# Two modulation part sums moved from product stages to two norms on TensorE

## The chip, the cores and the metric

The kernel runs on one core of a Trainium2 chip. The metric is the device time of one execution in microseconds (us), taken as the median of several runs. One core has a matmul engine (TensorE, called PE in the profile, with its weight loads shown apart as PEld), a vector engine (VectorE, DVE), a scalar engine (ScalarE, ACT), GpSimd (POOL) and SyncE (SP). The last two mostly issue transfers here.

## The reference, cut to what matters

Two transformer blocks of two layers each work on 256 tokens of width 1024; layer 0 has 256 context tokens beside them. Every layer is modulated by a vector computed from a condition:

```python
m_lat = jnp.split((cond_lat @ mod_w[layer] + mod_b[layer])[:, None, :], 6, axis=-1)   # first block
h_lat = modulate(rms_norm(x, norm_g[layer, 0]), m_lat[0], m_lat[1])                   # h * (1 + scale) + shift
...
x = x + m_lat[5] * swiglu(modulate(rms_norm(x, norm_g[layer, 1]), m_lat[3], m_lat[4]), ffn_w_in[layer], ffn_w_out[layer])
...
mod = c_act @ w_ada[l] + b_ada[l]                                                     # second block
```

Each of the four modulation matrices is 1024 x 6144. This is a product of one or two row vectors with a large matrix, and none of it depends on the tokens. All of it can be done at any time before the layer that needs it.

## The kernel before, in words

Every engine's program is written out by hand, in the order in which that engine runs it; semaphores join them. The token products fill PE nearly all the time.

The modulation is cut into twelve groups, three of 2048 columns for each of four layers (`MOD_GROUPS`, L220). Group 0 is made by PE from the weights. For groups 1 to 11 the matrix comes in 88 slabs of 128 rows, each 1 MB. DVE multiplies each slab with its piece of the condition and adds it up in an accumulator of 128 x 2048 (`mod_slabs`, L2966). What is left is the sum over the 128 partitions. PE makes it in `mod_sum` (L1430): products of a selecting matrix with the four quarters of the accumulator, 32 rows each, into one PSUM bank. ACT copies that bank to `mod_rows` (L2288). PE turns it in `mod_turn` (L1420) by four transposes, and ACT copies 16 columns out (L2297). From group 4 on, a sum waits for the columns of the group before it, since the bank and `mod_rows` are shared.

Where PE runs the sums and turns is set by three small tables:

- In the first feed-forward's down product, twelve chunks with seven products each, group 5 is summed at chunk 3 and group 6 at chunk 7 (`MOD_DOWN_SUM`). Each is turned one chunk later. ACT copies them from inside the squares for the next norm (L2661 to L2665).
- In the odd layer, jobs are counted: 12 value units (0 to 11), 8 query products, 8 key products. Groups 7 to 11 are summed after jobs 1, 4, 8, 20 and 25 (`MOD_SUM_AFTER`), and each is turned after the next job. Before the retention scores PE waits for all twelve columns (L2034).

A norm on PE (`norm`, L1466) adds up squares by products with a matrix of ones. ACT then makes the inverse root (Ln, Exp), DVE scales the eight blocks of x, ACT adds the shift, and the first products of the next stage wait for these blocks one by one. While the chain runs, PE makes constant products whose result nobody reads (`spare`, L1453), 3 of width 512 where the norm has 512 tokens and 2 where it has 256. Each f32 product of the program appears as two instructions in the trace.

The value units (`retention_values`) and the feed-forward (`seven_products`) use a seven-product scheme of the Strassen kind: 1, 2, 5, 6, 1 of the next, 7, and so on. ACT copies the results of products 1, 6 and 7 out, because product 6 is added on top of product 1 in the same PSUM bank, and product 7 on top of that. So product 6 of a unit waits for the copy of product 1 (L2604 in the feed-forward, L2686 in the value units), and product 7 for the copy of product 6 (L2609 and L2696). The weights come over the SP queue in a ring of tiles, each load waiting for the products that used the tile before.

Of the kernel before, what the change touches and what calls it, by code (L numbers as in the profile page):

```python
# [219 lines left out]
MOD_GROUPS = [(layer, g) for layer in range(4) for g in range(3)]  # L220
MOD_SUM_AFTER = {"even": (13,), "odd": (1, 4, 8, 20, 25)}
MOD_EARLY = 8
SP_SLABS = 36
MOD_UP_SUM, MOD_DOWN_SUM = {9: 3, 19: 4}, {3: 5, 7: 6}
MOD_UNITS, MOD_ODD = (1, 2, 3, 2, 3, 2, 3, 2, 0, 0, 0, 0), 14
# [5 lines left out]


DOWN_SLABS = (2, 2, 0, 3, 3, 0, 3, 3, 0, 2, 2, 0)

# [228 lines left out]
def first_then_second_block(nc, a, out):  # L463
# [3 lines left out]
    with ExitStack() as ctx:  # L467
# [575 lines left out]
        def _(pe):  # L1043
# [413 lines left out]

            def feed_forward_norm(use, width, name, f):

                def between():  # L1460
                    pe.wait_ge(st_e, 28 * f + 23)
                    nc.tensor.matmul(acc[:, 3, 0:256], ones, fconst[:, 0:256], start=True, stop=True)

                norm(use, width, name, (st_e, 28 * f + 22), between)

            def norm(use, width, name, free=None, between=None):  # L1466

# [13 lines left out]
                if use:  # L1481
                    spare(mx[:, 1, :], 3 if width == 512 else 2)
                fresh[0] = use
# [261 lines left out]

            def seven_products(f, use, width, up_name, down_name, ffT, mods=False, params=None, final=False):

# [78 lines left out]
                for q in range(1, KF):  # L1826
# [9 lines left out]
                    if mods and q in MOD_UP_SUM:  # L1836
                        mod_sum()
                    product3(q - 1)
                    product7(q)
# [188 lines left out]
            seven_products(0, 1, 512, "ffn0", "down0", ffT4, mods=True)  # L2028
            feed_forward_norm(2, 512, "norm2", 0)
            own.n = 0  # L2030
            retention_values(2)
            for lo in (256, 256, 0, 0):
                by_feature(4, lo, 512, where="odd")
            pe.wait_ge(mod_c, len(MOD_GROUPS))  # L2034
            def ret_scores(h):
# [25 lines left out]
            quadrants("ret_out", roT, 8, *turned_back("ret_oT", 2))  # L2061
            norm(3, 256, "norm3", (out_e, 28 * OUT_USE["ret_out"] + 23))
            seven_products(1, 3, 256, "ffn1", "down1", ffT2, params=0)


# [169 lines left out]
        def _(act):  # L2235
# [352 lines left out]

            def feed_forward(f, width, mods=False):

# [7 lines left out]
                for q in range(KF + 1):  # L2598
# [18 lines left out]
                    if mods and q in MOD_UP_SUM:  # L2617
                        mod_sum()
                    if q:
                        act.wait_ge(st_c00, pair0 + q)  # L2620
                        nc.scalar.activation(g0[:, 1 - b, 0:w], g0[:, 1 - b, 0:w], ACT.Silu).then_inc(st_g0, 1)
# [34 lines left out]
            def down0_done(block):  # L2656

                p = block // 2
                if block % 2 == 0:
                    if p == 1:  # L2660
                        mod_sum()  # L2661
                        mod_turn()
                    if p == 2:
                        mod_sum()
                        mod_turn()  # L2665
                    down_done(0, 512, block)
# [13 lines left out]
            for q in range(units + 1):  # L2680
# [6 lines left out]
                if q == 0:  # L2687
                    shifted(2, 512, first=10)
                if q >= 1:
                    act.wait_ge(rv_x, q)  # L2690
# [42 lines left out]
            norm(3, 256, "norm3", quadrants_done("ret_out", 8))  # L2733
            feed_forward(1, 256)

# [205 lines left out]
        def _(dve):  # L2941
# [811 lines left out]
            quadrants("ret_out", 2, roT, 8, 1, lambda: weights_summed(KF + 12, pl.tile["ffn1"], 4))  # L3753
            dve.wait_ge(mod_c, 12)

            def layer_params(l):

                dve.wait_ge(par_sb, 2 * l + 2)
                link(V.tensor_tensor(mb[:, l, 0, :], modc[:, 2 + l, 0, :], vcols[:, 48 * l + 128:48 * l + 176], ALU.add))
# [404 lines left out]
```

## Time and profile before

| | |
|---|---|
| median of 3 runs | 2548.81 us (2548.07 to 2548.89) |
| the profiled execution, whole | 2547.73 us |
| its span | 2545.9 us |
| PE busy | 2474.6 us, 97% |
| DVE busy | 1696.6 us, 67% |
| ACT busy | 659.2 us, 26% |

The span is the time from the first to the last instruction that the profiler saw; the whole execution has 1.8 us around it. Times in the timelines are counted from the start of the span. An entry in brackets gives how long the engine was idle before a row and what ended that.

### The profile page before, as it was taken

How to read it: one execution, taken by the hardware profiler on the slowest of the kernel's cores; microseconds unless marked ns; L12 is line 12 of the kernel's file. 1: busy time of each engine (PE TensorE's matmuls, PEld its weight loads, DVE VectorE, ACT ScalarE, POOL GpSimd, SP SyncE). 2: the span in 40 equal slices, each digit the busy share in tenths (PEclk: the TensorE clock that was granted, in tenths of full speed). 3: DMA queues.
4: the chain of work that ended last, by engine and by line, in shares of the span. 5: the costliest groups of instructions: out<-in, count | busy, mean ns of one | idle time of the engine just before them, and what ended most of it. 6: DMA issues, size and time to landing. Idle time of an engine off the chain costs nothing.

```text
span 2545.9 us, 41380 instructions
## 1 busy us (share of the span) xinstructions
PE 2474.6 (97%) x16822; PEld 2022.4 (79%) x16822; DVE 1696.6 (67%) x3326; ACT 659.2 (26%) x1768; POOL 73.2 (3%) x96
## 2 busy tenths in 40 slices
PE   6999899999999999999999999999999999999999
PEld 3544448888888886599998877869999877868999
DVE  4967767655877645466675777647776667648785
ACT  3145512111102111112212153333321135333320
POOL 0000000000000001100000001100000000110000
PEclk9999999999999999999999999999999999999999
DMA  8531115555575868335654424135653433124563
GB/s 342 189 117 42 51 34 182 151 179 166 190 272 176 288 213 312 89 114 160 174 167 150 152 80 133 68 112 143 171 174 129 156 124 108 68 90 143 166 179 121
DMA packets 342654, 386.80 MB, mean 152 GB/s; under 512 B 8111, under 2 KB 285191, under 8 KB 330177
## 3 DMA queue, kind: packets, MB, share of 16 engines
q1 hardware_dynamic: 330896, 320.89, 40.3%
q0 software_dynamic: 8832, 57.26, 6.3%
q10 hardware_dynamic: 2736, 6.01, 0.6%
q8 instruction: 134, 2.20, 0.4%
q14 instruction: 56, 0.45, 0.1%
HBM read 383.08 MB, written 1.05 MB: 151 GB/s over the span
## 4 chain that ended last, share of the span: by engine, by line
PE 83%; DVE 9%; ACT 3%; issue 3%; DMA 2%; ACTq 0%; DVEq 0%; SPq 0%
PE acc L1072 33%; PE mx L1072 16%; PE acc L1123 9%; PE acc L1111 7%; PE acc L1200 5%; PE acc L1696 2%; PE acc L1645 1%; PE mx L2054 1%; DMA ring<-in_odd_w_in 1%; DVE arena L4077 1%; PE mx L1505 1%; DVE hT L3017 1%; PE mx L2041 1%; PE mx L2113 1%; PE mx L1529 1%
## 5 line engine op out<-in xcount | busy, mean ns | idle before, releaser
L1072 PE MATMUL acc<-arena 128*128 128x128 f32 (+1 forms) x2248 | 353.8, 300 | 1.0 <-ACT gate L2614 0.5
L1072 PEld LDWEIGHTS acc<-arena 128*128 128x128 f32 x2248 | 309.9, 192 | 16.8 <-ACT gate L2614 0.9
L2985 DVE SCALAR_TENSOR_TENSOR arena<-mod_w,vcols,arena 128x2048 f32<-128x2048 f32 x98 | 228.4, 2348 | 57.9 <-DMA mod_w<-in_w_ada 43.3
L1123 PE MATMUL acc<-hT,ring 128*128 128x256 f32 (+1 forms) x1024 | 250.0, 406 | 1.5 <-DVE arena L3702 0.8
L1123 PEld LDWEIGHTS acc<-hT,ring 128*128 128x128 f32 x1024 | 193.9, 190 | 55.2 <-issue 29.4
L3378 DVE TENSOR_TENSOR arena<-ring 128x512 f32<-128x512 f32 (+1 forms) x136 | 91.7, 674 | 178.9 <-PE acc L1072 174.2
L1072 PE MATMUL acc<-hT,ring 128*128 128x128 f32 (+1 forms) x1368 | 206.1, 301 | 2.8 <-ACT hT L2362 1.4
L1072 PEld LDWEIGHTS acc<-hT,ring 128*128 128x128 f32 x1368 | 184.8, 191 | 16.1 <-issue 6.4
L1072 PE MATMUL acc<-arena,ring 128*128 128x128 f32 (+1 forms) x1256 | 194.2, 298 | 0.0
L1072 PEld LDWEIGHTS acc<-arena,ring 128*128 128x128 f32 x1256 | 171.1, 192 | 7.7 <-issue 0.8
L1072 PE MATMUL mx<-hT,ring 128*128 128x128 f32 (+1 forms) x1152 | 174.2, 296 | 1.4 <-ACT arena L2650 0.9
L1072 PEld LDWEIGHTS mx<-hT,ring 128*128 128x128 f32 x1152 | 154.8, 192 | 7.9 <-ACT arena L2650 1.2
L1072 PE MATMUL mx<-arena,ring 128*128 128x128 f32 (+1 forms) x960 | 152.7, 301 | 0.0
L1072 PE MATMUL acc<-hT,arena 128*128 128x128 f32 (+1 forms) x888 | 141.0, 302 | 0.0
L1111 PE MATMUL acc<-ring,hT 128*128 128x512 f32 x320 | 138.7, 593 | 1.3 <-ACT hT L2271 1.3
L1072 PEld LDWEIGHTS mx<-arena,ring 128*128 128x128 f32 x960 | 132.8, 191 | 8.2 <-issue 2.5
L1072 PEld LDWEIGHTS acc<-hT,arena 128*128 128x128 f32 x888 | 123.6, 191 | 6.0
L1111 PEld LDWEIGHTS acc<-ring,hT 128*128 128x128 f32 x320 | 60.3, 190 | 76.5 <-issue 72.5
L1200 PE MATMUL acc<-ring,hT 128*128 128x256 f32 x384 | 96.4, 388 | 2.0 <-DVE arena L3897 0.7
L3382 DVE TENSOR_TENSOR arena<-ring 128x512 f32<-128x512 f32 (+1 forms) x136 | 92.0, 676 | 4.7
L3384 DVE TENSOR_TENSOR arena<-ring,arena 128x512 f32<-128x512 f32 (+1 forms) x136 | 92.0, 676 | 4.6
L1696 PE MATMUL acc<-hT,ring 128*128 128x512 f32 x192 | 90.6, 608 | 1.5 <-ACT arena L2271 1.5
(563 smaller groups left out, 3926.6 us busy)
## 6 DMA issues: line engine op xcount, KB each, us to landing
ring<-in_w_in SPq DMA_DIRECT2D x28, 2048.0 KB
mod_w<-in_w_ada POOLq DMA_DIRECT2D x48, 1024.0 KB, 5.3
ring<-in_ffn_w_in SPq DMA_DIRECT2D x88, 512.0 KB
ring<-in_w_up SPq DMA_DIRECT2D x88, 512.0 KB
mod_w<-in_mod_w SPq DMA_DIRECT2D x36, 1024.0 KB, 4.9
ring<-in_odd_w_in SPq DMA_DIRECT2D x20, 1024.0 KB
ring<-in_ffn_w_out SPq DMA_DIRECT2D x16, 1024.0 KB
ring<-in_w_down SPq DMA_DIRECT2D x16, 1024.0 KB
```

Source lines behind the costliest of these rows:

```text
L1072: ins = nc.tensor.matmul(out, w[:, k, :], h[:, k, :], start=start and k == 0, stop=stop and k == n - 1, skip_group_check=more)
L1111: ins = nc.tensor.matmul(b[:, 0:width], src[:, k, P * i:P * (i + 1)], w[:, k, :], start=k == 0, stop=k == KD - 1)
L1123: ins = nc.tensor.matmul(b[:, 0:hi - lo], w[:, k, P * f:P * (f + 1)], hT[:, k, lo:hi], start=k == 0, stop=k == KD - 1)
L1200: ins = nc.tensor.matmul(out, a_[:, k, :], b[:, k, :], start=first and k == 0, stop=last and k == 3, skip_group_check=True)
L1505: ins = nc.tensor.matmul(mx[:, v, 0:P * (i + 1)], sqT[half, j, P * i:P * (i + 1)], skT[half, 0:P * (i + 1)], start=True, stop=True)
L1529: ins = nc.tensor.matmul(mx[half, 3, 0:P], s_v[:, b, half], pPT[o % 2][:, at:at + P], start=b == 0, stop=b == n - 1)
L1645: ins = nc.tensor.matmul(b, w[:, k, P * f:P * (f + 1)], src[:, k, :], start=k == 0, stop=k == 3)
L1696: ins = nc.tensor.matmul(hb, hw[:, kk, P * j:P * (j + 1)], hT[:, kk, :], start=kk == 0, stop=kk == KD - 1)
L2985: ins = V.scalar_tensor_tensor(acc_, mod_w[:, i % 2, :], vcols[:, at:at + 1], acc_, ALU.mult, ALU.add)
L3378: V.tensor_tensor(s3, a11, a10, ALU.subtract)
L3382: link(V.tensor_tensor(s2, a11, a10, ALU.subtract))
L3384: V.tensor_tensor(s4, a01, s2, ALU.subtract).then_inc(st_ws, 1)
```

## The change

The sum of group 6 leaves the down product and goes into the norm ahead of the value units (norm2), behind one of the three constant products; the other two are gone. It is turned after value unit job 0. The sum of group 11 leaves job 25 and goes into the norm ahead of the second feed-forward (norm3), behind one of the two constant products; the other is gone. It is turned at q = 2 of that feed-forward. ACT copies group 6 after the last shifts of norm2, ahead of the copy of product 6 of unit 0, and group 11 after the last shift of norm3, ahead of the table load of the feed-forward. The waits for the last group's columns move back accordingly.

```diff
-MOD_SUM_AFTER = {"even": (13,), "odd": (1, 4, 8, 20, 25)}
+MOD_SUM_AFTER = {"even": (13,), "odd": (-1, 1, 4, 8, 20)}
-MOD_UP_SUM, MOD_DOWN_SUM = {9: 3, 19: 4}, {3: 5, 7: 6}
+MOD_UP_SUM, MOD_DOWN_SUM = {9: 3, 19: 4}, {3: 5}
+LAST_TURN = 2
...
-            def norm(use, width, name, free=None, between=None):
+            def norm(use, width, name, free=None, between=None, sums=False):
...
                 if use:
-                    spare(mx[:, 1, :], 3 if width == 512 else 2)
+                    spare(mx[:, 1, :], 1 if sums else 3 if width == 512 else 2)
+                if sums:
+                    mod_sum()
...
+                    if q == turn:
+                        mod_turn()
                     product3(q - 1)
...
-            feed_forward_norm(2, 512, "norm2", 0)
+            feed_forward_norm(2, 512, "norm2", 0, sums=True)
...
-            pe.wait_ge(mod_c, len(MOD_GROUPS))
+            pe.wait_ge(mod_c, len(MOD_GROUPS) - 1)
...
-            norm(3, 256, "norm3", (out_e, 28 * OUT_USE["ret_out"] + 23))
-            seven_products(1, 3, 256, "ffn1", "down1", ffT2, params=0)
+            norm(3, 256, "norm3", (out_e, 28 * OUT_USE["ret_out"] + 23), sums=True)
+            seven_products(1, 3, 256, "ffn1", "down1", ffT2, params=0, turn=LAST_TURN)
...
-            def feed_forward(f, width, mods=False):
+            def feed_forward(f, width, mods=False, turn=None):
...
+                    if q == turn:
+                        mod_turn()
                     if q:
                         act.wait_ge(st_c00, pair0 + q)
...
                     if p == 1:
-                        mod_sum()
-                        mod_turn()
-                    if p == 2:
                         mod_sum()
                         mod_turn()
...
                 if q == 0:
                     shifted(2, 512, first=10)
+                    mod_sum()
...
             norm(3, 256, "norm3", quadrants_done("ret_out", 8))
-            feed_forward(1, 256)
+            mod_sum()
+            feed_forward(1, 256, turn=LAST_TURN)
...
-            dve.wait_ge(mod_c, 12)
 
             def layer_params(l):
 
+                dve.wait_ge(mod_c, len(MOD_GROUPS))
                 dve.wait_ge(par_sb, 2 * l + 2)
```

## Rows read from the trace of the kernel before

**Rows 1.** Page: busy time by engine; chain that ended last, by engine.

```profile
PE 2474.6 (97%) x16822; PEld 2022.4 (79%) x16822; DVE 1696.6 (67%) x3326; ACT 659.2 (26%) x1768; POOL 73.2 (3%) x96
...
PE 83%; DVE 9%; ACT 3%; issue 3%; DMA 2%; ACTq 0%; DVEq 0%; SPq 0%
```

**Rows 2.** Timeline, PE, down product: start, length, line, operands, count.

```profile
738.41 1.89 PE L1072 MATMUL acc<-arena,ring 128*128 128x256 f32 x8
740.23 1.07 PE L1439 MATMUL mx<-arena,cond 128*32 128x512 f32 x8
741.22 1.99 PE L1072 MATMUL mx<-arena,ring 128*128 128x256 f32 x8
743.05 1.89 PE L1072 MATMUL acc<-arena,ring 128*128 128x256 f32 x8
...
751.69 1.89 PE L1072 MATMUL acc<-arena,ring 128*128 128x256 f32 x8
753.41 0.60 PE L1426 MATMUL mx<-fconst,mod_rows 128*128 128x128 f32 x4
753.85 1.46 PE L1072 MATMUL mx<-arena,ring 128*128 128x256 f32 x6
```

**Rows 3.** Timeline, key products: the sum and turn of group 11.

```profile
1023.71 4.46 PE L1123 MATMUL acc<-hT,ring 128*128 128x512 f32 x10
...
1029.09 7.13 PE L1123 MATMUL acc<-hT,ring 128*128 128x512 f32 x16
1029.22 0.60 ACT L2288 ACTIVATE mod_rows<-mx 128x512 f32<-128x512 f32 x1 [0.43 <-PE mx L1439]
...
1036.49 4.03 PE L1123 MATMUL acc<-hT,ring 128*128 128x512 f32 x9
```

**Rows 4.** Timeline, norm2 and the first value unit.

```profile
799.16 2.74 PE L1456 MATMUL mx<-fconst 128*128 128x512 f32 x6
...
801.92 1.97 PE L1072 MATMUL acc<-ring,hT 128*128 128x256 f32 x8
...
807.79 1.99 PE L1072 MATMUL acc<-arena 128*128 128x256 f32 x8 [0.28 <-DVE arena L3658]
808.17 2.50 ACT L2362 ACTIVATE hT<-hT,mb 128x256 f32<-128x256 f32 x6 [2.53 <-DVE hT L3017]
...
809.63 1.89 PE L1072 MATMUL acc<-ring,hT 128*128 128x256 f32 x8
...
810.58 0.36 ACT L2696 ACTIVATE x<-acc 128x256 f32<-128x256 f32 x1
...
811.35 1.89 PE L1072 MATMUL acc<-arena 128*128 128x256 f32 x8
```

**Rows 5.** Timeline, norm3 and the first products of the second feed-forward.

```profile
1142.86 1.88 PE L1456 MATMUL mx<-fconst 128*128 128x512 f32 x4
...
1145.26 2.49 PE L1072 MATMUL acc<-hT,ring 128*128 128x128 f32 x16 [0.52 <-ACT hT L2362]
...
1147.93 1.28 ACT L2321 ACT_TABLE_LOAD   x1
...
1149.23 0.28 ACT L2604 ACTIVATE gate<-acc 128x128 f32<-128x128 f32 x1
...
1149.75 1.06 PE L1072 MATMUL acc<-arena 128*128 128x128 f32 x8
```

**Rows 6.** Chain that ended last: start, length, what; two weight loads.

```profile
902.84 1.74 PE acc L1072 x8
...
904.60 7.92 DMA ring<-in_odd_w_in
...
1103.23 9.30 DMA ring<-in_odd_w_out
```

**Rows 7.** Windows: length, PE, PEld, DVE, ACT, POOL busy, PEclk, DMA share, GB/s.

```profile
24.00:26.00 2.00, 1.02 (x10) 0.78 (x8) 1.97 (x5) 2.00 (x6) 0.00 (x0) 1.00 0.98 414
...
2540.00:2546.00 6.00, 1.81 (x15) 1.38 (x13) 1.92 (x7) 0.60 (x1) 0.00 (x0) 0.92 0.13 44
```

More of the change, by code:

```diff
@@ L1456, in spare, with feed_forward_norm @@
                     nc.tensor.matmul(out, ones, fconst[:, 0:out.shape[1]], start=True, stop=True)
-            def feed_forward_norm(use, width, name, f):
+            def feed_forward_norm(use, width, name, f, sums=False):
                 def between():
@@ L1462, in between @@
                     nc.tensor.matmul(acc[:, 3, 0:256], ones, fconst[:, 0:256], start=True, stop=True)
-                norm(use, width, name, (st_e, 28 * f + 22), between)
-            def norm(use, width, name, free=None, between=None):
+                norm(use, width, name, (st_e, 28 * f + 22), between, sums)
+            def norm(use, width, name, free=None, between=None, sums=False):
                 stage(name)
@@ L1744, in store_pair, with seven_products @@
                 ins.then_inc(out_ps, 1)
-            def seven_products(f, use, width, up_name, down_name, ffT, mods=False, params=None, final=False):
+            def seven_products(f, use, width, up_name, down_name, ffT, mods=False, params=None, final=False, turn=None):
                 w = width // 2
```

## The prediction

> **What bounds the kernel now.** I read the page first: the busy times and the chain that ended last. PE is busy for 97% of the span, and 83% of that chain is PE's own work [rows 1]. So an instruction that leaves PE is worth its issue time, unless the place it leaves has another limit. Which limit that is must be read place by place, so I went through the timeline of PE at the four places that the change touches: the down product from chunk 7 on, norm2 with unit 0, the key products, and norm3 with the first products of the second feed-forward. Then I read ACT there, since ACT takes over two copies inside the norms, and last the weight loads on the chain, where a gain could be swallowed.
>
> **Part 1: what leaves the product stages.** In the down product one product follows the other every 1.73 us without a gap. From 738.41 to 743.05 there are 4.64 us for two products with the sum of group 6 between them, so the sum costs 4.64 - 2 x 1.73 = 1.18 us [rows 2]. Its turn costs 753.85 - 751.69 - 1.73 = 0.43 us [rows 2]. In the key products an instruction of width 512 is issued every 0.43 us (ten of them last 4.46, the last alone some 0.59, so nine steps take 3.87). From 1023.71 to 1036.49 there are 26 of them, 11.18 us, in 12.78 us, so the sum and turn of group 11 cost 1.60 us together, 1.17 for the sum and 0.43 for the turn [rows 3]. Both places are bound by PE: no bracket with a wait stands before any of these rows, and DVE and ACT follow PE there. What is late next after the removal is again PE's next product. The sums thus take off 1.18 + 1.17 = 2.35 us. The waits inside the sums (slabs added up, previous columns there) never held PE in these rows, and both sums now come later, so they don't hold it in the norms either.
>
> **Part 2: the turns.** They are moved, not removed. Group 6 is turned behind unit job 0, among products of width 256 as before, and group 11 at q = 2 among products of width 128. PE is the limit in both stages too. I put 0.43 us back for each, that is a change of 0.0 in all; a place with an unseen gap could give up to 0.4 back, and a restart behind it could cost 0.1. ACT's copy out of a turn is one small instruction between copies that all wait for PE.
>
> **Part 3: the sums in the norms, on PE.** In norm2 six constant instructions, three products, are issued in 6 x 0.43 = 2.57 us from 799.16 on. Then the first product starts at 801.92 with the first shifted block [rows 4]. After the change there are 0.86 us of constant products and 1.18 of the sum: PE is free at 801.20, sooner than now. In norm3 four constant instructions end their issue at 1144.58, and the first product waits 0.52 us for ACT's shift until 1145.26 [rows 5]. After the change PE is free at 1142.86 + 0.86 + 1.18 = 1144.90, still 0.36 us before the shift. Both sums cost nothing on PE: their cover is the chain through ACT and DVE. Without that cover the one in norm3 would cost 1.18 - 0.86 = 0.32.
>
> **Part 4: the copies on ACT.** This is what the change adds to the path. Copying a summed bank takes 0.60 us [rows 3]. In norm2 it stands behind the last shifts and ahead of the copy for product 7 of unit 0. The shifts end at 810.67 less an overlap, ACT goes straight on at 810.58, and this copy ends at 810.94, 0.4 us before product 7 starts at 811.35 without a wait [rows 4]. With 0.60 in between it ends at 811.54, and product 7 can start some 0.05 later, at 811.6. A product that restarts behind a wait takes 0.11 longer to its follower, as 807.79 to 809.63 = 1.84 against 1.73 shows [rows 4]. So this costs 811.59 + 0.11 - 811.35 = 0.35 us. The bounds are 0.1 (the weight load of product 7 goes ahead during the wait, and ACT's instructions overlap by 0.05 to 0.1) and 0.6 (nothing of the copy is hidden). In norm3 it stands ahead of the table load. The copy of product 1 now ends at 1149.51 and product 6 starts at 1149.75 [rows 5]. The new end is 1150.11, product 6 starts at 1150.16, and it costs 0.41 us, or 0.45 with the restart at width 128. The bounds are 0.2 and 0.7. Together I take 0.35 + 0.45 = 0.80 us. Behind these two products nothing else is late. Unit 0 and q = 0 merely shift, and DVE gets more time. The queues of SP and POOL issue nothing more or less than before. Their loads wait for products, so they shift with PE.
>
> **Part 5: fewer constant products.** They keep PE at work while the norm runs. The sum works on 32 columns of the array at a time. PE's clock is granted in full in nearly every window, also where PE works only 1.02 of 2 us; it reads 0.92 only at the very end, where PE has stopped for good [rows 7]. The change leaves PE without work for some 0.7 us in norm2 (now 0.2) and 0.4 in norm3. That is less than the 0.98 us missing in the window at 24 us, where the clock stayed full, and I put nothing down for it. A rule that speaks against the change is on the page "TensorE: Matmul & The Clock Gate" of the Trainium skill, Part 1: the gate halves PE's clock unless the array has been busy lately. By the row the sum stays as it is; by that rule, if the thinner work counted as idleness, the clock case below would come in. Its time is worked out there from rows.
>
> **The sum.** -2.35 (two sums) + 0.0 (two turns) + 0.0 (PE in the norms) + 0.80 (two ACT copies) = -1.55 us. Against its own profiled execution, 2547.73 us of which 2545.9 are the span, this gives 2546.2. That execution lies 1.08 under the median of the runs, so I set the sum against the median as well, 2548.81 - 1.55 = 2547.3, and forecast that.
>
> **The rivals.**
> - **The copies are hidden, or not at all.** At their lower bounds they cost 0.3, the time is 2548.81 - 2.05 = 2546.8; fully hidden it is 2546.5. At their upper bounds, 1.3, it is 2547.8. For it: the margins that I work with are 0.2 to 0.4 us. This moves the time within the same verdict.
> - **Weight loads swallow the gain; slower.** On the chain stand a load of 7.92 us at 904.60 and one of 9.30 us at 1103.23 [rows 6]. If their landings were set by something that doesn't shift with PE (slabs on the same DMA engines, say), whatever is gained ahead of each would be lost in the wait. Then the 1.18 of group 6 and the 1.60 of group 11 would be gone, and what comes behind the second load would remain as a loss: 0.45 at norm3 and 0.43 for the turn, 2548.81 + 0.88 = 2549.7. It decides from a landing that stays in place while PE comes over 0.75 us sooner. Against it: the first load starts right where a product ends, 902.84 + 1.74 = 904.58, so its start shifts with PE [rows 6]. Only contention could hold the landing. Half of it would give about 2548.5.
> - **The clock falls in a norm; slower.** If the thinner work let the clock drop from 2.4 to 1.2 GHz ahead of unit 0, its seven products would take 7 x 1.73 = 12.1 us more. The time would be 2547.3 + 12.1 = 2559.4, and with a few products only some 2552. It decides once three products run at half speed. The rows at full clock with longer gaps speak against it [rows 7]. This is also what the page's rule would give here.
> - **The change doesn't do what it says.** The sums could be held in a norm by a wait. The slabs of group 6 are read long before norm2, and those of group 11 before job 25, where the sum ran without a wait [rows 2, 3]. So I give this hardly anything; each us of it would add a us.
>
> **How the numbers follow.** The forecast with its neighbours on the ACT copies has 0.80, the loads 0.10, the clock 0.04, the rest, a changed alignment of transfers that no row shows, 0.06, of either sign. 0.2% of this kernel, 5.1 us, is about what a measurement can tell from no change. The forecast and the loads lie inside that; the clock case is mostly slower; the rest could be 5 us either way in a few cases. That gives 0.03 faster, 0.92 same, 0.05 slower. The range takes in the bounds of the copies, the load case at 2549.7, and about 0.8 us beneath the hidden copies for the difference between builds: 2545.7 to 2549.8.
>
> **What would show it.** In the profile after: no L1439 row in the chunks after 3 and in the key products, with the products there 1.73 and 0.43 apart right through. Two constant instructions and eight of the sum in each norm. The first product of norm2 and norm3 as long after the norm's last product of ones as now. In unit 0, product 7 with a bracket naming ACT L2696, and product 6 of q = 0 in the second feed-forward with one naming L2604, each 0.3 to 0.5 us late. PE's clock at 1.00 in both. At 912 and 1112 us PE 0.8 and 2.4 us earlier. The forecast is wrong if the first product of a norm comes later, if those two brackets are missing or longer than 0.7, or if the wait for weights near 912 grows by what was gained.

## The result and the profile after

The changed kernel took 2551.26 us (median of 13 runs, 2546.52 to 2555.04), the kernel before, on the same chip, 2547.25 (13 runs, 2544.78 to 2549.71). The ratio is 1.0016, with a 95% interval of 1.0009 to 1.0024: slower by 4 us, where 1.55 us less had been forecast. The 13 times of after fall apart, six from 2546.5 to 2549.7, one at 2551.3 and six from 2553.6 to 2555.0 at a mean granted clock of 0.997 or 0.998, while of the kernel before none of these 13 took over 2550, and 20 of its 157 in five later sessions did. The profiled execution took 2554.8 us, its span 2552.9. It is one of the six longest, so its trace shows more loss than the 4 us between the medians.

What was moved looks as forecast. This is PE's timeline of after in norm2 and the first value unit (start, length, line, operands, count, idle time before it and what ended it), to be held against [rows 4]:

```profile
799.09 1.02 PE L1457 MATMUL mx<-fconst 128*128 128x512 f32 x2
800.04 1.07 PE L1440 MATMUL mx<-arena,cond 128*32 128x512 f32 x8
801.84 1.97 PE L1073 MATMUL acc<-ring,hT 128*128 128x256 f32 x8 [0.74 <-ACT hT L2365]
...
809.54 1.89 PE L1073 MATMUL acc<-ring,hT 128*128 128x256 f32 x8
...
811.39 1.99 PE L1073 MATMUL acc<-arena 128*128 128x256 f32 x8
813.23 1.89 PE L1073 MATMUL acc<-ring,gate 128*128 128x256 f32 x8
```

PE stands idle for 0.74 us between the sum and the first shifted block. The product behind it starts 2.75 us after the first constant product, as before (2.76). The copies on ACT behind it, in the same kernel:

```profile
808.09 2.51 ACT L2367 ACTIVATE hT<-hT,mb 128x256 f32<-128x256 f32 x6 [2.53 <-DVE hT L3023]
810.49 0.58 ACT L2293 ACTIVATE mod_rows<-mx 128x512 f32<-128x512 f32 x1
810.97 0.37 ACT L2701 ACTIVATE x<-acc 128x256 f32<-128x256 f32 x1
```

In norm3 the picture is the same, against [rows 5]:

```profile
1148.26 1.02 PE L1457 MATMUL mx<-fconst 128*128 128x512 f32 x2
1149.21 1.07 PE L1440 MATMUL mx<-arena,cond 128*32 128x512 f32 x8
1150.66 2.49 PE L1073 MATMUL acc<-hT,ring 128*128 128x128 f32 x16 [0.38 <-ACT hT L2367]
```

The loss lies between the two norms, at the waits for two weight loads: the one ahead of product 1 of the tenth value unit, and the one ahead of the third group of key and query products. PE's timeline of the kernel before at both places, and the two loads on its chain (one of them stands in [rows 6]):

```profile
912.56 1.99 PE L1072 MATMUL acc<-ring,hT 128*128 128x256 f32 x8 [1.08 <-DMA ring<-in_odd_w_in]
915.02 3.72 PE L1072 MATMUL acc<-ring,gate 128*128 128x256 f32 x16 [0.47 <-DVE ring L3655]
918.58 1.89 PE L1072 MATMUL acc<-arena,gate 128*128 128x256 f32 x8
...
985.06 7.13 PE L1123 MATMUL acc<-hT,ring 128*128 128x512 f32 x16 [0.72 <-DMA ring<-in_odd_w_in]
...
970.60 14.42 DMA ring<-in_odd_w_in
```

The same of after, timeline and chain:

```profile
915.62 3.68 PE L1073 MATMUL acc<-ring,hT 128*128 128x256 f32 x8 [3.56 <-DMA ring<-in_odd_w_in]
919.14 3.62 PE L1073 MATMUL acc<-ring,gate 128*128 128x256 f32 x16
922.59 1.89 PE L1073 MATMUL acc<-arena,gate 128*128 128x256 f32 x8
...
990.72 7.54 PE L1124 MATMUL acc<-hT,ring 128*128 128x512 f32 x13 [2.37 <-DMA ring<-in_odd_w_in]
...
905.18 10.40 DMA ring<-in_odd_w_in
...
974.62 16.06 DMA ring<-in_odd_w_in
```

And the windows of after there (length, busy time of PE, PEld, DVE, ACT and POOL, then PEclk, DMA share, GB/s):

```profile
912.00:914.00 2.00, 0.06 (x1) 0.00 (x0) 0.00 (x0) 0.38 (x1) 0.00 (x0) 1.00 1.06 375
914.00:916.00 2.00, 0.38 (x1) 0.38 (x2) 0.33 (x1) 0.00 (x0) 0.00 (x0) 0.93 1.09 347
916.00:918.00 2.00, 2.00 (x6) 1.55 (x6) 2.00 (x2) 0.00 (x0) 0.00 (x0) 0.50 0.22 73
918.00:920.00 2.00, 2.00 (x8) 1.65 (x7) 1.93 (x3) 0.38 (x1) 0.00 (x0) 0.72 0.00 0
920.00:922.00 2.00, 2.00 (x11) 1.76 (x10) 1.55 (x4) 0.00 (x0) 0.00 (x0) 1.00 0.03 8
...
990.00:992.00 2.00, 1.28 (x2) 0.76 (x3) 1.50 (x1) 1.11 (x1) 0.00 (x0) 0.70 0.93 361
992.00:994.00 2.00, 2.00 (x3) 0.71 (x3) 0.85 (x1) 0.00 (x0) 0.53 (x1) 0.50 1.02 423
994.00:996.00 2.00, 2.00 (x6) 0.80 (x5) 0.99 (x1) 0.00 (x0) 0.00 (x0) 0.95 1.00 386
```

The reader is to see three things. Both loads started when PE's products let them, and took 2.5 and 1.6 us longer. PE stood idle for 3.56 and 2.37 us instead of 1.08 and 0.72. And behind each wait the granted clock went to 0.50, which is 1.2 GHz, for about one product: eight instructions of width 256 lasted 3.68 us in place of 1.99. At the first load 0.7 of the 1.7 us was hidden, because before has a wait for DVE behind that product (2.46 us from its start to the next one's in place of 1.73) and after has not. From its start to that of the third behind it there are 918.58 - 912.56 = 6.02 us in before and 922.59 - 915.62 = 6.97 in after. So the first load cost 2.5 + 0.95 us and the second 1.65 + 1.7, which makes 6.8 us in this execution. The rest of the 7.0 us between the two spans nearly cancels: 1.55 was lost ahead of the change already (the same product starts at 675.38 in before and at 676.93 in after), the down product gave back 1.6 and the key products 1.6, the turns and ACT's copies cost 1.5, a third load came 0.3 sooner, 0.5 more came back up to 2240 us, and 1.2 us were lost in a stage of small products near 2250, where the DMA engines are nearly idle (their share is 0.01) and PE's clock is full. There after has two gaps that the profile calls "issue" and before has none:

```profile
2247.55 0.27 PE L2186 MATMUL mx<-arena 64*64 64x64 f32 x1 [0.34 <-issue]
...
2251.04 0.27 PE L2186 MATMUL mx<-arena 64*64 64x64 f32 x2 [0.37 <-issue]
...
2248.00:2252.00 4.00, 3.55 (x146) 3.06 (x137) 2.91 (x12) 0.77 (x2) 0.00 (x0) 1.00 0.01 4
```

The last line is the window there. The experiments come back to this place at their end.

### The profile page after: what moved, and what is told of

It is laid out like the page before. It is cut to its first block, busy times and chain, and to the rows that moved or that the text cites. A ratio compares the mean times of both kernels' runs of the same rounds, so it can differ in the third digit from the quotient of the medians.

```text
span 2552.9 us, 41368 instructions
## 1 busy us (share of the span) xinstructions
PE 2477.2 (97%) x16816; PEld 2023.5 (79%) x16816; DVE 1696.3 (66%) x3326; ACT 658.3 (26%) x1768; POOL 73.0 (3%) x96
## 4 chain that ended last, share of the span: by engine, by line
PE 78%; DVE 11%; DMA 4%; issue 3%; ACT 3%; SPq 0%; ACTq 0%; DVEq 0%
PE acc L1073 33%; PE mx L1073 16%; PE acc L1124 9%; PE acc L1201 5%; PE acc L1112 3%; DMA mod_w<-in_mod_w 2%; PE acc L1699 2%; PE acc L1648 1%; DVE arena L2991 1%; PE mx L2059 1%; DMA ring<-in_odd_w_in 1%; DVE arena L4083 1%; PE mx L1508 1%; DVE hT L3023 1%; PE mx L2046 1%
```

## The experiments

Each was timed beside the kernel before on the same chip. "Mean" is that of all 11 or 12 runs, without one run of 3196 us (one constant product in norm2) and one of 7288 us (the kernel before); the ratio, its interval in brackets, leaves these two out as well. The sessions were on different chips, so each version is compared with the kernel before of its own session. The waits are those of the one profiled execution of each version. The first load is the one at 912 us, the second the one at 985.

### First: which half of the change

The whole change again, word for word:

> The changed kernel itself, once more, as the measure for the three beside it. Theory 1 (load and clock): its times fall in two groups, one within 2 us of the kernel before and one some 5 to 7 us above the lower, and an execution of the upper group has a granted clock 0.001 to 0.002 lower; in the profile the wait for odd_w_in near 912 us is 2.5 us or more when the product behind it runs at half clock (3.7 us for its eight instructions in place of 1.9), and 1 to 2 us when it does not. Theory 2 (a chance of the first measurement): one group only, median within 1 us of the kernel before.

Measured: median 2550.02, mean 2549.1, ratio 1.0006 (0.9997 to 1.0014): less than the first time, and this interval alone takes in no change. The profiled execution showed the first load once more, and no such clock at the second (2.2 us of wait at full clock):

```profile
913.07 3.78 PE L1073 MATMUL acc<-ring,hT 128*128 128x256 f32 x8 [2.86 <-DMA ring<-in_odd_w_in]
```

Only group 11 moved (group 6 stays at chunk 7):

> Group 11 alone is moved to norm3; group 6 is summed and turned in the down product as in the kernel before, and norm2 has its three constant products. Theory 1 (moving group 6 shifts PE against the slabs and makes the wait for weights near 912 us longer, until the clock falls): no fall of the clock at 912, time 0.7 us below the kernel before (-1.6 for sum and turn in the key products, +0.43 for the turn at q = 2, +0.45 for the copy on ACT). Rival (moving group 11 does the harm): 3 to 4 us above the kernel before. Rival (both are harmless and the loads land by chance): same as the changed kernel's spread.

Measured: median 2545.91, mean 2546.1, ratio 0.9991 (0.9983 to 1.0000), 1.6 us under the median of before in that session. The first load is waited for 0.6 us, the second not at all.

Only group 6 moved:

```diff
-MOD_SUM_AFTER = {"even": (13,), "odd": (1, 4, 8, 20, 25)}
+MOD_SUM_AFTER = {"even": (13,), "odd": (-1, 1, 4, 8, 20, 25)}
...
-MOD_UP_SUM, MOD_DOWN_SUM = {9: 3, 19: 4}, {3: 5, 7: 6}
+MOD_UP_SUM, MOD_DOWN_SUM = {9: 3, 19: 4}, {3: 5}
...
```

> Group 6 alone is moved to norm2; group 11 is summed after job 25 and turned after job 26 as in the kernel before, and norm3 has its two constant products. Theory 1: the loss is here: 3 to 5 us above the kernel before in the median, two groups of times, the wait near 912 us 2.5 us or more in a slow execution and the next product at half clock. Rival (group 11 does the harm): 0.9 us below the kernel before (-1.6 + 0.43 + 0.25).

Measured: median 2550.95, mean 2550.1, ratio 1.0008 (0.9999 to 1.0017). The times fall apart as in the whole change, five from 2546.7 to 2547.1 and seven from 2550.9 to 2554.4. Its profile had 1.94 us of wait at the second load and the clock at 0.50 behind it. So the harm comes with group 6 (4.0 us between the means of these two versions in one session), and group 11 gives what was forecast for it: 1.60 less 0.43 for the turn and 0.45 for the copy would be 0.7, and 1.6 were seen, the rest within the noise.

The whole change with slabs 72 and 73 requested two steps later, behind the value units:

```diff
-MOD_UNITS, MOD_ODD = (1, 2, 3, 2, 3, 2, 3, 2, 0, 0, 0, 0), 14
+MOD_UNITS, MOD_ODD = (1, 2, 3, 2, 3, 2, 3, 0, 0, 0, 0, 0), 16
```

> The changed kernel with the two slabs of value unit 7 (numbers 72 and 73) added up after the units instead, so that no slab is asked for between the unit's product and the weight load near 905 us. Theory 1 (the load lands late because slabs share the DMA engines): the wait near 912 us falls under 1 us and nothing there runs at half clock; the time is 3 to 5 us below the changed kernel. Rival (the load is late for another reason): the wait stays at 2.5 us or more and the time does not fall; two slabs more behind the units could then lengthen the second load's wait near 985 us.

Measured: median 2546.57, mean 2546.4, ratio 0.9995 (0.9987 to 1.0004). No wait at the first load; 2.63 us at the second, at full clock. So the first load's wait comes from these slabs: without them it is gone. That fits slabs and weights passing through the same DMA engines, which were busy all the time there (the share of 1.06 in the window at 912).

### Second: turn, copies, cover

The kernel before with four transposes more behind unit job 0:

> The kernel before with four more transposes behind unit job 0, whose result nobody reads: PE is 0.43 us later from unit 1 on against the slabs that were asked for before, and nothing else of the change is in. Theory 1a (the shift of PE against the slab loads puts the weight loads in a worse phase): the waits for weights near 912 and 985 us grow to 2 to 3 us in the profile, the median is 2 to 3 us above the kernel before. Theory 1b (it is not that shift): the time is 0.4 us above the kernel before, waits near 1.1 and 0.7.

Measured: median 2547.66, ratio 1.0003 (0.9994 to 1.0012), waits of 0.8 and 0.3 us. PE's later arrival by a turn is not the cause.

The whole change with both ACT copies one step later (behind the copy of product 6 in unit 0, behind that of product 1 at q = 0):

> The changed kernel with ACT's two copies of summed banks one step later: group 6 behind the copy of product 6 of unit 0, group 11 behind the copy of product 1 of q = 0. The 0.24 us (unit 0) and 0.44 us (second feed-forward) that products 7 and 6 start late in the changed kernel's trace are gone: PE has no bracket with a wait for them, 0.7 us less. Theory 1 (phase of the loads): the first 0.24 come back in front of the loads, the two groups of times may shift in their shares. Rival (the copies do the harm): the time falls to 1.6 us below the kernel before and the upper group is gone.

Measured: median 2550.16, mean 2549.3, ratio 1.0011 (1.0002 to 1.0020). Products 7 and 6 restart without the delay (808.61 to 810.34 is 1.73), but the first load is waited for 2.96 us, with the clock at 0.50 behind it. The copies aren't the cause either.

The whole change with two constant products ahead of each of the two waits, as cover for the clock:

```diff
+                    if q == 9:
+                        spare(mx[:, 2, :], 2)
                     product1(q)
...
+            for n, lo in enumerate((256, 256, 0, 0)):
+                if n == 2:
+                    spare(mx[:, 2, :], 2)
```

> The changed kernel with two constant products of width 512 (four instructions, 1.72 us) ahead of each of the two products that wait for weights near 912 and 985 us. They lie inside the wait where it is longer than 1.72 us. Theory 1 (after a wait of about 3 us the clock falls to 1.2 GHz and the next products take 1.7 us more): no product behind these waits runs at half clock, the idle gap is under 2 us, the executions of the upper group come down by 1.7 us for each fall, and the median is 0 to 2 us below the changed kernel. Rival (the clock has no part): each execution is up to 1.7 us longer for each wait that is shorter than 1.7 us, and none is shorter.

Measured: median 2548.47, mean 2548.2, ratio 1.0003 (0.9994 to 1.0012). In the profiled execution the wait stays and the clock stays full. By itself this doesn't price the clock: the eight further instructions also change the number of those that follow, which the fourth and fifth set turn to.

```profile
909.78 1.88 PE L1457 MATMUL mx<-fconst 128*128 128x512 f32 x4
913.75 1.99 PE L1073 MATMUL acc<-ring,hT 128*128 128x256 f32 x8 [2.09 <-DMA ring<-in_odd_w_in]
```

Group 11 alone moved, with the slabs later:

> Group 11 alone is moved to norm3, and the slabs 72 and 73 are added up behind the units, as in the earlier run with the whole change. Theory 1: the wait near 912 us is under 0.6 us in every execution and moving only group 11 has its gain of some 1 us: 1 to 3 us below the kernel before, the lowest of all so far, no upper group. Rival (the loads behind the units get the two slabs more in their way): the wait near 985 us grows to 2 us or more, and the time is the kernel before's.

Measured: median 2543.36, mean 2542.9, ratio 0.9985 (0.9976 to 0.9994). Neither load is waited for. This is the fastest version of all that were run, 3.6 us under the median of the kernel before.

### Third: the parts of group 6's move

Its turn alone moved to unit job 0, the sum left at chunk 7:

> The kernel before, in which group 6 is still summed at chunk 7 of the down product (on PE and on ACT), but turned behind unit job 0, PE and ACT. Nothing else moves; norm2 keeps its three constant products. Theory 1 (what lengthens the two weight loads is that the down product gets shorter ahead of norm2 or that norm2 has thinner work on PE): the turn alone does nothing, the first load's wait stays at 0.6 to 1.2 us, the second's at 0.3 to 0.7, and the time is that of the kernel before, ratio 1.0000 within 0.0006. Rival 2 (the later turn and its copy, with the sums of groups 7 to 9 that wait for it, are what changes the place of the slabs): waits of 1.5 us and more at one of the loads, ratio 1.0010.

Measured: median 2546.28, ratio 0.9997 (0.9989 to 1.0006), waits of 1.2 and 0.9 us at full clock.

The kernel before with one constant product in norm2:

```diff
-                    spare(mx[:, 1, :], 3 if width == 512 else 2)
+                    spare(mx[:, 1, :], (1 if use == 2 else 3) if width == 512 else 2)
```

> The kernel before with one constant product in norm2 in place of three, so that PE has 1.7 us less to do while the norm runs; nothing moves and nothing of the result changes. Theory 1a (the thinner norm is what costs: PE's clock or its restart behind the norm): ratio 1.0008 or more, the two weight waits at 1.5 us or more. Theory 1b (the shorter down product is what costs): the time of the kernel before, within 0.0006, and its waits.

Measured: median 2550.70, ratio 1.0014 (1.0005 to 1.0023); the lowest of its runs is 2549.5. Nothing of the modulation is moved here, the first product of unit 0 still starts 2.76 us after the first constant product, and yet 3.7 us are lost. The profiled execution waited longer than the kernel before at both loads (1.6 and 2.3 us, full clock), which makes 2.1 us, and lost another 1.1 in the stage near 2250:

```profile
799.68 1.02 PE L1456 MATMUL mx<-fconst 128*128 128x512 f32 x2
802.44 1.97 PE L1072 MATMUL acc<-ring,hT 128*128 128x256 f32 x8 [1.73 <-ACT hT L2360]
...
913.60 1.99 PE L1072 MATMUL acc<-ring,hT 128*128 128x256 f32 x8 [1.60 <-DMA ring<-in_odd_w_in]
...
987.68 2.84 PE L1123 MATMUL acc<-hT,ring 128*128 128x512 f32 x6 [2.30 <-DMA ring<-in_odd_w_in]
```

The kernel before with the slabs later:

> The kernel before with slabs 72 and 73 requested two steps later, behind the value units; no sum and no turn moves. Splits the gain of the version that moved group 11 and these slabs (2542.95 mean against 2547.36). If the slabs are what the first weight load waits for (theory 1), its wait of about 1 us goes and the ratio is 0.9992, and group 11 gave the rest (some 1.5 to 2 us). If the gain needs both, the ratio is 1.0000 within 0.0004.

Measured: median 2544.92, mean 2544.7, ratio 0.9990 (0.9981 to 0.9999), no wait at either load. The gain of the fastest version (3.6) is this one's (2.1) and group 11's (1.6).

Group 6 moved, with constant products in the down product in place of its sum and turn:

```diff
+                    if mods and n in (7, 8):
+                        pe.wait_ge(mod_c, 6)
+                        for w_ in ((512, 128) if n == 7 else (256,)):
+                            spare(mx[:, 3, 0:w_], 1)
```

> Group 6 alone moved, as in the version with that part alone (2550.14 mean against 2547.98), with constant products put into the down product in the place of its sum (widths 512 and 128, chunk 7) and of its turn (width 256, chunk 8), so that norm2 starts as late as before. Theory 1b (the norm and what hangs on it starts 1.6 us sooner against the transfers, and that lengthens the loads): the longer waits go, the first 0.5 to 1.2 us, the second under 0.8, and what is left is the turn and the ACT copy in unit 0, +0.4 to +0.8 us, ratio 1.0002 to 1.0003. Theory 1a or any other cause: the waits of the moved group 6 stay (1.9 us and more at one load, with half clock behind it in some executions), ratio 1.0010 or more.

Measured: median 2547.93, mean 2547.9, ratio 1.0003 (0.9995 to 1.0012), waits of 0.5 us and none. That fits the theory that the earlier start of norm2 does the harm. But the version with one constant product in norm2, which starts that norm as late as the kernel before does, was slow too, so that theory can't be the whole. What both slow versions lack, and this one has again, is something else: instructions in PE's program.

### Fourth: work or count

Each f32 product is two instructions in the trace. The page of before counts 16822 matmul instructions, that of after 16816: two constant products are gone from norm2 and one from norm3, while the sums' 8 and the turns' 4 only move. So behind the turn of group 6 the whole change is four short, and so is the version with one constant product in norm2. Two readings were left: PE's thin work in norm2, or the place of all later instructions in PE's program.

The same work in norm2, six instructions more (six constant products of width 256):

> The kernel before, in which the three constant products of width 512 in norm2 are six of width 256: the same 2.6 us of work, six more instructions in PE's program. Theory A (thin work of PE in norm2 is what costs the 3.7 us): the time of the kernel before, ratio 1.0000 within 0.0005. Rival B (any change of the number of instructions ahead of the value units moves what follows in PE's program, and the time with it): a ratio away from 1 by 0.0007 or more, of either sign.

Measured: median 2547.37, ratio 0.9996 (0.9988 to 1.0005). The rival as written there, that any change of the number shows, fell: six instructions more cost nothing.

The thin work of norm2 with the count of before (three constant products of width 170):

> The kernel before, in which the three constant products of norm2 have width 170 in place of 512: 0.9 us of work in place of 2.6, as in the version with one constant product, but the number of instructions is that of the kernel before. Theory A: ratio 1.0012 to 1.0016, with waits of 1.5 us and more at one of the two weight loads. Rival B: the time of the kernel before, ratio 1.0000 within 0.0005.

Measured: median 2547.23, ratio 0.9998 (0.9989 to 1.0006), waits of 0.7 and 0.5 us:

```profile
799.47 1.03 PE L1456 MATMUL mx<-fconst 128*128 128x170 f32 x6
802.22 1.97 PE L1072 MATMUL acc<-ring,hT 128*128 128x256 f32 x8 [1.73 <-ACT hT L2363]
```

PE has the same 1.03 us of work and the same 1.73 us without any as in the slow version, and nothing is lost. The thin work is not the cause: the version with one constant product, run beside it, had a mean 2.1 us above this one's (2549.2 against 2547.1).

The version with one constant product again:

> The version with one constant product in norm2 again, word for word, beside the two above. Both theories: 2550.5 to 2551.5 us, ratio 1.0012 to 1.0016. If it comes out within 0.0006 of 1, the earlier 1.0014 was no property of the kernel (theory C: an alignment that changes from one session of runs to the next).

Measured: median 2549.47, mean 2549.2, ratio 1.0001 (0.9992 to 1.0010). It met neither side cleanly: by the medians 2.2 us slower than the kernel before, by the ratio the same. Its profiled execution (2549.3 us) waited for 0.5 and 0.8 us at the two loads, no more than the kernel before. What it shares with the first run's is the stage near 2250, again 1.2 us longer. So late loads don't come with this version each time.

The whole change with two constant products in norm2:

> The whole change with two constant products of width 512 in norm2 in place of one, ahead of the sum. PE then works 1.71 + 1.18 = 2.89 us in the norm, 0.13 more than the 2.76 from the first constant product to the first shifted block in the kernel before. Theory A: what the change lost to the thinner norm comes back: 2546.5 to 2547.5 us, ratio 0.9996, no long wait and no half clock at the two loads. Rival B or C: the time of the whole change, ratio 1.0006 to 1.0016, with waits of 2 us and more.

Measured: median 2546.11, mean 2545.9, ratio 0.9990 (0.9982 to 0.9999), waits of 0.2 and 0.6 us, full clock. The gain that the change should have brought is there: 1.15 us by the medians, 1.8 by the means.

### Fifth: the count alone, and the candidate

The whole change with two further constant products of width 32 in norm2:

```diff
                     spare(mx[:, 1, :], 1 if sums else 3 if width == 512 else 2)
+                if use == 2:
+                    spare(mx[:, 1, 0:32], 2)
                 if sums:
                     mod_sum()
```

> The whole change with two further constant products of width 32 in norm2: next to no work (some 0.1 us), but four more instructions in PE's program ahead of the value units, so that it has as many up to the turn of group 6 and behind it as the kernel before. Rival B (the place of the later instructions in PE's program): 2545.5 to 2547 us, ratio 0.9992 to 0.9998, no half clock at the two loads. Theory A' (the work of PE in the norm, which the version with two constant products of width 512 had put back): the time of the whole change, ratio 1.0006 to 1.0016, with waits of 2 us and more at a load.

Measured: median 2545.55, mean 2545.9, against 2546.89 and 2547.2; ratio 0.9994 (0.9985 to 1.0003). The additions are worth 0.37 us of PE's time (1.39 in place of 1.02), and no wait of over 1 us for the two loads is left (0.91 and none):

```profile
795.94 1.39 PE L1457 MATMUL mx<-fconst 128*128 128x512 f32 x6
797.25 1.06 PE L1440 MATMUL mx<-arena,cond 128*32 128x512 f32 x8
798.69 1.97 PE L1073 MATMUL acc<-ring,hT 128*128 128x256 f32 x8 [0.37 <-ACT hT L2367]
...
909.82 1.35 PE L1073 MATMUL acc<-ring,hT 128*128 128x256 f32 x5 [0.91 <-DMA ring<-in_odd_w_in]
```

The whole change with two constant products and the slabs later:

> The whole change with two constant products in norm2 (2545.9 mean against 2547.7) and slabs 72 and 73 two steps later, the candidate for the best version. If both gains add (slabs -2.6, change -1.8) it comes to 2543, ratio 0.9983. If the moved group 6 stays harmful at the second load, as with one constant product and these slabs later (2546.4), ratio 0.9992 to 0.9996.

Measured: median 2545.20, mean 2545.8, ratio 0.9995 (0.9986 to 1.0004), with 1.3 us of wait at the second load. The gains don't add: with the slabs behind the units, group 6's move costs some 3 us (2545.8 and 2546.4 in the means with both groups moved, 2542.9 with group 11 alone).

### What the runs say together

Matmul instructions of PE's program up to and with the turn of group 6, against the kernel before, with the slabs where they were:

| versions | instructions | medians, us | ratios |
|---|---|---|---|
| whole change (twice), group 6 alone, copies later | -4 | 2551.26, 2550.02, 2550.95, 2550.16 | 1.0016, 1.0006, 1.0008, 1.0011 |
| one constant product in norm2 (twice) | -4 | 2550.70, 2549.47 | 1.0014, 1.0001 |
| whole change with cover at the waits | -4, 0 behind the first cover, +4 behind the second | 2548.47 | 1.0003 |
| whole change, two constant products | -2 | 2546.11 | 0.9990 |
| whole change, two narrow ones added | 0 | 2545.55 | 0.9994 |
| group 11 alone, turn alone, narrow (170) products | 0 | 2545.91, 2546.28, 2547.23 | 0.9991, 0.9997, 0.9998 |
| down product filled, dummy turn, six products of 256 | +2, +4, +6 | 2547.93, 2547.66, 2547.37 | 1.0003, 1.0003, 0.9996 |

By the medians the two kinds don't overlap, nor by their distance from the kernel before of the same session (2.2 to 4.0 us above it for the first two rows, 1.5 above to 1.6 below for the others). The order was seen only after the third set, though, and by the ratios the second run of norm2 with one constant product lies among the others. Two runs were made to test it, the width of 170 and the two narrow products, and both came out as it said. That it is the count of instructions, or what hangs on it, and not the work, is therefore supported, with one repeat that is unclear.

One part of the loss goes with the count in every trace. The stretch of PE's program that lasts from 2240.3 to 2256.2 us in the kernel before holds the same products in all 20 traces. It takes 15.93 to 15.95 us in the eleven whose page counts 16820 matmul instructions or more, and 16.96 to 17.83 in the nine with 16818 or fewer. These nine are the six of the table's first two rows, the whole change with two constant products, and those with the slabs later that move both groups. (Group 11's move alone takes two off in norm3 and stays at 15.93.) The loss of 1.0 to 1.9 us lies at gaps called "issue", as in the two lines of after above and in the second run of norm2 with one constant product:

```profile
2245.66 0.27 PE L2179 MATMUL mx<-arena 64*64 64x64 f32 x1 [0.61 <-issue]
```

The profile's queues suggest what the engine waits for there. From the page of after (packets, MB, share of 16 engines):

```profile
q1 hardware_dynamic: 330896, 320.89, 40.3%
q8 instruction: 134, 2.20, 0.4%
```

The instructions come over the same DMA engines, 2.20 MB in 134 packets, 16.4 KB each. The Trainium skill says how ("Runtime: NRT & Kernel Launch", Instruction fetch mechanics): an engine's sequencer fetches its program in blocks of 16 KiB, or 256 instructions, while it executes the one before. The packet size agrees. Where the blocks begin then depends on how many instructions stand ahead. The page also calls the cost of a fetch mostly hidden, and near 2250 it seems not to be. No view gives these packets a time, but the traces keep it: in after two packets landed at 2246.36 and 2249.76, and PE went on behind its two gaps at 2247.55 and 2251.04, 1.2 and 1.3 us later. In the repeat with one constant product a packet landed at 2244.39 and PE went on at 2245.66. The first packet inside the stretch starts 2.6 to 3.1 us behind its beginning in the nine traces and 0.7 to 1.5 us behind it in the eleven. A late instruction fetch is therefore the likely reading for this part. No run moved a block boundary there on purpose.

How the count would reach the two loads is not shown. The same packet times rule out that an instruction packet meets the first load: in every trace in which PE waits for it the last one starts 17 us or more before the load, and the next one after it has landed. What goes with the length of that load is when POOL asks for its second slab beside it, behind DVE's slab 73. These are the requests in before, where the load starts at 904.60, and in after, where it starts at 905.18:

```profile
903.69 0.53 POOL L984 DMA_DIRECT2D mod_w<-in_w_ada  x1 [1.93 <-DVE arena L2985]
...
905.50 0.53 POOL L985 DMA_DIRECT2D mod_w<-in_w_ada  x1 [1.93 <-DVE arena L2991]
```

In eleven traces this request comes 0.15 to 1.0 us ahead of the load, which then takes 7.3 to 8.4 us. In four, the whole change twice, with the copies later and with cover, it comes 0.3 to 1.0 us behind, and the load takes 9.7 to 10.6. In one, with two constant products, it comes 2.4 us behind, and the load takes 7.0. So the order of requests on the full DMA engines fits the first load, though no run changed that order alone, and why it turns in these versions stays open. The second load stays open as well. In the six traces where it took 15.0 to 16.3 us an instruction packet started 0.9 to 1.6 us behind its start. In seven of the eight where it took 14.0 to 14.6 the packet came ahead of it, but in the kernel before it came 1.3 us behind.

## Why the prediction was wrong, point by point

Two steps failed. The prediction let the weight loads "shift with PE", and they took 2.5 and 1.6 us longer, with the clock at half behind them. And it put nothing down for the constant products that it took away, whose number came with a loss of 1.0 to 1.9 us near 2250 in every trace and with a long load in five of the six traces of such versions. How the number reaches the loads stays open.

- **Part 1, the sums, right.** The rows of the sum and the turn are gone from the down product and the key products. From the product at 675 us to the first product of unit 0 after gained 1.63 us on before (1.55 behind, then 0.08 ahead), where 1.18 + 0.43 = 1.61 were reckoned.
- **Part 2, the turns, right.** In norm3's stage the turn at q = 2 and the copy together lost 0.87 us up to 1357, against 0.43 + 0.45.
- **Part 3, the sums hidden in the norms, right.** 0.74 and 0.38 us to spare on PE, forecast 0.72 and 0.36. The first products started as soon behind the norm's last product of ones as before.
- **Part 4, the copies, right in kind and a little too high in size.** Product 7 of unit 0 came 0.13 later and its follower another 0.11 (813.23 - 809.54 = 3.69, before 3.45 with 813.08 from the same view), 0.24 in place of 0.35. At q = 0 it was 0.44 in place of 0.45.
- **Part 4, last sentence, wrong.** "Their loads wait for products, so they shift with PE" holds for where the loads start and not for how long they take. 7.92 us became 10.40 and 14.42 became 16.06. The prediction took the length of a transfer, on DMA engines that were full, as a constant of the load.
- **Part 5, wrong in its result.** It asked whether fewer constant products could cool PE in the norm, answered rightly that they don't (1.73 us of idleness at full clock), and put nothing down for them. Their removal yet came with the harm, by another way: with their number restored at almost no work the change gained 1.34 us by the medians, with one more of full width 1.15, against 1.55 reckoned.
- **The rival of the weight loads, right place, wrong mechanism, and with 0.10 too small.** It decided from a landing that stays in place while PE comes sooner, and was priced at +0.9 us, for a wait that swallows a gain. Against the product at 675 us PE had gained 1.0 us up to the first load, and the wait grew by 2.5. So the landing moved back by more than the gain, and PE's clock came on top of it.
- **Part 5, the clock, misread.** The last window is not the only low one. In the same trace the windows from 234 to 238 and from 309 to 313 us read 0.54 to 0.60, behind idle times of 1.87 and 1.86 us. Less than 2 us without work can thus come before a fall, which the row at 24 us seemed to deny:

```profile
233.59 0.63 PE L1666 MATMUL mx<-fconst,arena 128*128 128x128 f32 x4 [1.87 <-ACT arena L2539]
...
234.00:236.00 2.00, 2.00 (x6) 0.51 (x4) 1.93 (x6) 1.97 (x4) 0.00 (x0) 0.54 0.00 0
```

- **The rival of the clock, right size, wrong place.** A product at 1.2 GHz costs 1.7 us more, as written. It was looked for in the norms, and it came behind the waits for weights, where PE had stood idle for 2 to 3.6 us. The two rivals were treated as exclusive, and here one brought on the other.
- **The range** ended at 2549.8, the load rival's time. With one load 2.5 us later and one product at half clock behind it, of which 1.0 stays, it would have reached 2547.3 + 2.5 + 1.0 = 2550.8. The base was high as well, 2548.81 from three runs against 2547.25 from 13, so against the kernel beside it the forecast was missed by 5.6 us (4.0 and 1.55). The move stayed inside 0.2%, as forecast, with the other sign.

## What to carry to other kernels

Where PE waits for a load even by 1 us in the profile before, that load has no slack left, so price it with the clock behind it, not alone, and look at what else its DMA engines carry. Here moving two slabs out of its way was worth more (2.1 us by the medians) than taking the sums off PE. An edit that changes the number of instructions on the busiest engine can move the time by as much as the edit itself is worth (here 1.0 to 1.9 us in one stage alone); before it is judged, run it once with the count restored by a few tiny instructions.

## What was not expected of the hardware

- PE's clock fell to 1.2 GHz behind waits of 3.56, 2.96, 2.86, 2.37 and 1.94 us, and stayed full behind waits of 2.63, 2.30, 2.18 and 2.09. In the kernel before it fell behind idle times of 1.87 and 1.86 us. The length of the wait alone doesn't decide it. The fall near 309 us is in all 20 traces, the one near 235 in seven and one near 282 in two more. An execution without the one near 235 is some 1.65 us ahead behind that place, so part of the spread between executions comes from there.
- One and the same load took 7.0 to 10.6 us (the first) and 14.0 to 16.3 us (the second) in different versions.
- Two constant products of width 512 fewer, in a place where PE then has 1.73 us of nothing to do and is late for nothing, made the kernel slower by 3.7 and 2.2 us by the medians of two sessions (ratios 1.0014 and 1.0001, the second not clear of noise).
- PE stood still for up to 0.9 us at a time near 2250 us, with its clock full, the DMA engines at 0.01 of their time and nothing named that it waited for, in just the versions with 16818 matmul instructions or fewer.
